# The causal convolution of a hybrid decoder layer, with tokens on the partitions

## Chip, cores and metric

One core of a Trainium2 chip runs the whole program. The metric is the device time of one execution in microseconds (us), lower is better; the kernel before takes 1735.56 us (median of 3 runs, 1734.17 to 1737.68). The engines are PE (TensorE, matmuls and transposes), DVE (VectorE), ACT (ScalarE), POOL (GpSimd) and SP (SyncE, which here only issues transfers). Sixteen DMA engines move data. SBUF is the on-chip memory with 128 partitions, PSUM the one that PE writes.

## What is computed

Two layers on x of 256 tokens by 2048 features. What the change touches is the convolution group.

```python
h = _rmsnorm(x, norm_pre) * (1.0 + scale[:, None, :]) + shift[:, None, :]
z = h @ w_in                                  # 2048 x 14336
gb, gcin, u, g_c, q, k, v, g_r = jnp.split(z, offs, axis=-1)

y_conv = gb * _causal_short_conv(gcin * u, conv_w)   # sum of w[k] * up[:, k:k + s], 3 taps over tokens
y_conv = y_conv * jax.nn.silu(g_c)
...                                           # rope, retention with 8 heads, GroupNorm, silu(g_r): y_ret
o = jnp.concatenate([y_conv, y_ret], axis=-1) @ w_out
return x + gate[:, None, :] * _rmsnorm(o, norm_post)
```

All data are float32. The scale, shift and gate come from silu(c) @ w_ada, also with 2048 x 6144 weights a layer.

## The kernel before

**Weights.** The work is a list of chunks `CH`. A chunk is 512 weight rows by 512 columns (1 MB; the 35 chunks at the front are of other sizes). SP loads it into one of 4 slots of `stage` (L528 to L545), in an order fixed by `load_table`; a slot is loaded again once what was in it is used. ACT casts each half chunk to float32r, `w_hi` (`cast`, L569), DVE subtracts to get the rest, `w_lo` (`low`, L744), and PE forms three products for each pair of tiles (`products`, L1162 to L1164): activations and weights are both split in a high and a low part. `w_hi` and `w_lo` are rings of 4 half chunks, so a cast waits for PE's products of two chunks before. Slots of `stage` also take parts of `w_ada`, 1 MB each, that DVE multiplies and adds itself (`ada_chunk`, L763 and L765): in turns 1, 2 and 3 for layer 1, and in the output projections.

**Turns.** The columns of `w_in` are worked through in 4 turns a layer, 8 in all (t = 0 to 7), each with 512 columns of each of 7 blocks (q and k, v, g_r, g_c in, u, g, gb), 28 chunks a turn, 4 to a block. Layer 0's turn 0 is spread over the front. Beside the products of a chunk each engine runs one small piece of the turn, chosen by a hand-written timetable: `Steps_at` holds for each piece at which chunk, counted from the turn's first, it stands in each engine's program. `USUAL` is for turns 1 to 7, `FIRST` for turn 0. A step above 27 lies in the chunks of the next turn (or of the output projection). All engines run their programs in order, and at every chunk an engine does first the cast, `low` or products of that chunk, then a `w_ada` part where there is one, and then the pieces of that step. In turn 0 the steps count from chunk 28, so steps 7 and on lie beside turn 1's first chunks.

**The convolution.** `z` has tokens on the partitions (tile i has tokens 128 i to 128 i + 127), in PSUM, or in `part` for turn 0. In order:
- `cu` (DVE, step 21; 8 in turn 0): u times g_c in, into `R2` (or `part`), still by tokens.
- `trc` (PE, 21; 9): eight 128x128 transposes into PSUM bank B (A in turn 0), so that features are on partitions and tokens along the row.
- `y0` (ACT, 23; 11): last tap into `R4`, four activations with a scale for each partition (L721). In turn 0 it waits for `s_in`, the products of the retention (PE's `inner`, step 9), as in the others.
- `conv` (DVE, 24; 12): the taps one and two tokens back, eight multiply-adds on shifted rows (L1038).
- `sg` (ACT, 25; 9) silu(g) and `gate` (DVE, 29; 10) gb times it, by tokens, in `R2`; `trg` (PE, 29; 21): eight transposes of that.
- `ymul` (DVE, 31; 23): gate times convolution, in `R4`; `yhi` (ACT, 32; 24) and `ylo` (DVE, 33; 25) split it into `YC` for the output projection.

The steps of the retention lie between: `rope` 5, `p` 9, `inner` 9, `stats` 11, `yn` 13 and so on. `R4` also takes the retention's scores `p` from turn 2 on.

Of the kernel before, what the change touches and what calls it, by code (L numbers as in the profile page):

```python
# [10 lines left out]
F32 = mybir.dt.float32  # L11
# [53 lines left out]
def chunk_table():  # L65
# [7 lines left out]
    for l in range(LAYERS):  # L73
# [5 lines left out]
        for nb in range(NB):  # L79
            for w in range(OUT_CH):  # L80
# [39 lines left out]
                for kc in range(tiles)]  # L120
# [15 lines left out]
                      " gcopy cu trc y0 conv sg gate trg ymul yhi ylo")  # L136
# [83 lines left out]
def build(nc, x, c, positions, norm_pre, norm_post, w_ada, b_ada, w_in, conv_w, gn_gain, w_out,  # L220
          consts, decay, out):
    ctx = ExitStack()
    with ctx:
# [62 lines left out]
        front_stage, _ = place("front_stage", [P, SLOTS, CK, BLK], F32, at_yr)  # L286
        c_cols, _ = place("c_cols", [P, KT, COL], F32, at_r4)
# [69 lines left out]
        s_trc = sem("cu_transposed")  # L357
        s_y0 = sem("conv_last_tap")
# [100 lines left out]
        def cu_bank(t):  # L459
            return four(A if t == 0 else B)  # L460
# [100 lines left out]
        def _(act):  # L561
# [77 lines left out]
            for n, ch in enumerate(CH):  # L639
# [35 lines left out]
                for t in turn_of(n):  # L675
# [8 lines left out]
                    if s == at.v and t > 0:  # L684
                        act.wait_ge(s_pe, z_done(t, VV))
                        act.wait_ge(s_in, t)
                        N.copy(v_sb[:, :, :], z_of(t, VV)).then_inc(taken(t, VV)[0], 1)
# [7 lines left out]
                    if s == at.yn:  # L695
                        act.wait_ge(s_rs, t + 1)
                        act.wait_ge(s_trq, t + 1)
                        for q in range(4):
                            h, i = divmod(q, 2)
                            ins = N.activation(yn_buf(t)[:, i, h * DV:(h + 1) * DV], B[:, h, i * DV:(i + 1) * DV],  # L700
                                               ACT.Identity, bias=nb4[:, q:q + 1], scale=rs4[:, q:q + 1])
                        ins.then_inc(s_yn, 1)
                    if s == at.yrhi:
# [10 lines left out]
                    if s == at.y0:  # L714
                        act.wait_ge(s_trc, t + 1)
                        act.wait_ge(s_in, t + 1)
                        if t:
                            act.wait_ge(s_ylo, t)
                        for e in range(TILES):
                            w = PRM_CW + 48 * (t // TURNS) + KT * (CONV_K - 1) + 4 * (t % TURNS) + e  # L720
                            ins = N.activation(R4[:, e, :], cu_bank(t)[:, e, :], ACT.Copy, scale=prm[:, w:w + 1])  # L721
                        ins.then_inc(s_y0, 1)
# [14 lines left out]
        def _(dve):  # L737
# [108 lines left out]
            def x_end(i):  # L846

                dve.wait_ge(s_xsq, 2 + 2 * i + 2)
                variance(xsq[:, i, :], NT + i)

# [54 lines left out]
            for n, ch in enumerate(CH):  # L905
# [68 lines left out]
                for t in turn_of(n):  # L974
# [58 lines left out]
                    if s == at.conv:  # L1033
                        dve.wait_ge(s_y0, t + 1)
                        for back in (1, 2):
                            for e in range(TILES):
                                w = PRM_CW + 48 * (t // TURNS) + KT * (CONV_K - 1 - back) + 4 * (t % TURNS) + e
                                ins = V.scalar_tensor_tensor(R4[:, e, back:S], cu_bank(t)[:, e, 0:S - back],  # L1038
                                                             prm[:, w:w + 1], R4[:, e, back:S], ALU.mult, ALU.add)
                                if back == 1:  # L1040
                                    me.then(ins)
                            if back == 1:
                                me.wait()
                        ins.then_inc(s_cv, 1)
                    if s == at.gate:
                        if t == 0:
                            dve.wait_ge(s_fin, fin(GB))
                        else:
                            dve.wait_ge(s_pe, z_done(t, GB))
                            dve.wait_ge(s_trc, t + 1)  # L1050
                        dve.wait_ge(*taken(t, GG))
                        V.tensor_tensor(gate_buf(t), z_of(t, GB), sg_buf(t), ALU.mult).then_inc(taken(t, GB)[0], 1)
                    if s == at.ymul:
                        dve.wait_ge(s_trg, t + 1)
                        dve.wait_ge(s_cv, t + 1)
                        V.tensor_tensor(R4[:, :, :], gate_bank(t), R4[:, :, :], ALU.mult).then_inc(s_ym, 1)
                    if s == at.ylo:
                        dve.wait_ge(s_yhi, t + 1)
                        k = slice(4 * (t % TURNS), 4 * (t % TURNS) + 4)
                        V.tensor_tensor(YC[:, k, S:2 * S], R4[:, :, :], YC[:, k, 0:S].bitcast(F32), ALU.subtract)\  # L1060
                            .then_inc(s_ylo, 1)
# [7 lines left out]
        def _(pool):  # L1069
# [42 lines left out]

            for t in range(ALL_TURNS):
                pool.wait_ge(s_mv, t + 1)
                if t:
                    pool.wait_ge(s_yn, t)
# [15 lines left out]
        def _(pe):  # L1132
# [111 lines left out]
            for n, ch in enumerate(CH):  # L1244
# [32 lines left out]
                for m, at_n in enumerate(ADA_SUM):  # L1277
                    if n == at_n:
# [3 lines left out]
                        if s < USUAL.scores:  # L1282
                            pe.wait_ge(s_ym, t)
# [12 lines left out]
                for t in turn_of(n):  # L1296
                    at, s = steps(t), n - base(t)
                    if s == at.trq:
                        pe.wait_ge(s_rope, t + 1)
                        if t == 0:  # L1300
                            pe.wait_ge(s_tmp, group_units(0, GROUPS - 1))
                        else:
                            pe.wait_ge(s_cv, t)
                            pe.wait_ge(s_yn, t)
                        if t == TURNS:
                            pe.wait_ge(s_tmp, group_units(1, GROUPS - 1))
                        turned(four(B), tok(R1)).then_inc(s_trq, 1)
# [30 lines left out]
                    if s == at.trc:  # L1338
                        pe.wait_ge(*taken(t, UU))
                        if t:  # L1340
                            pe.wait_ge(s_yn, t + 1)
                        else:
                            pe.wait_ge(s_p, 1)
                        if t == 1:
                            pe.wait_ge(s_ym, 1)
# [42 lines left out]
```

## Time and profile before

| | |
|---|---|
| median of 3 runs | 1735.56 us (1734.17 to 1737.68) |
| the profiled execution's own time | 1735.0 us |
| its span, first to last instruction | 1733.1 us |
| TensorE's granted clock, mean | 0.995 of full |
| PE, DVE, ACT busy | 1696.5, 1130.0, 720.9 us |
| moved by DMA | 414.61 MB, 239 GB/s over the span |

The profile is of one execution. Busy times count instructions in execution; PE's matmuls are pipelined, so an instruction's time (0.39 us) is longer than the distance to the next (0.23 us). A row of a timeline gives start, duration, engine, line, operation, output and inputs and, in brackets, how long the engine was idle before and what released it. A row with "x4" is four instructions merged. Times from issue to landing are those of transfers.

### The profile page before, as it was taken

How to read it: one execution, taken by the hardware profiler on the slowest of the kernel's cores; microseconds unless marked ns; L12 is line 12 of the kernel's file. 1: busy time of each engine (PE TensorE's matmuls, PEld its weight loads, DVE VectorE, ACT ScalarE, POOL GpSimd, SP SyncE). 2: the span in 40 equal slices, each digit the busy share in tenths (PEclk: the TensorE clock that was granted, in tenths of full speed). 3: DMA queues.
4: the chain of work that ended last, by engine and by line, in shares of the span. 5: the costliest groups of instructions: out<-in, count | busy, mean ns of one | idle time of the engine just before them, and what ended most of it. 6: DMA issues, size and time to landing. Idle time of an engine off the chain costs nothing. (4 is left out here: it accounts for less than half of the span.)

```text
span 1733.1 us, 19029 instructions
## 1 busy us (share of the span) xinstructions
PE 1696.5 (98%) x7795; PEld 1385.5 (80%) x7795; DVE 1130.0 (65%) x1305; ACT 720.9 (42%) x814; POOL 40.9 (2%) x78
## 2 busy tenths in 40 slices
PE   5999999999999999999989999999999999999998
PEld 3667888888888888888868888888888888888886
DVE  2598766878787775677775545555554555467776
ACT  2333444443444444344354443444444444444332
POOL 4000000000000000000000000000000000000000
PEclk9999999999999999999999999999999999999999
DMA  9998545787878866777765555555555555568774
GB/s 341 383 379 307 190 165 195 250 290 269 296 269 290 291 235 233 267 281 282 279 226 170 177 194 188 176 180 191 194 176 194 185 184 173 188 234 298 285 281 186
DMA packets 227398, 414.61 MB, mean 239 GB/s; under 512 B 7520, under 2 KB 48880, under 8 KB 226544
## 3 DMA queue, kind: packets, MB, share of 16 engines
q1 hardware_dynamic: 225888, 408.97, 68.2%
q10 hardware_dynamic: 1424, 4.43, 0.6%
q8 instruction: 61, 1.00, 0.2%
q14 instruction: 25, 0.20, 0.0%
HBM read 411.28 MB, written 2.10 MB: 239 GB/s over the span
## 5 line engine op out<-in xcount | busy, mean ns | idle before, releaser
L744 DVE TENSOR_TENSOR w_lo<-stage,w_hi 128x1024 fp32r<-128x1024 f32 x574 | 692.7, 1222 | 519.7 <-ACT w_hi L569 517.9
L569 ACT CAST w_hi<-stage 128x1024 fp32r<-128x1024 f32 x574 | 596.4, 1051 | 947.0 <-PE Z L1164 605.5
L1162 PE MATMUL Z<-w_hi,H 128*128 128x512 f32 x1784 | 704.7, 395 | 8.5 <-DVE w_lo L744 5.8
L1164 PE MATMUL Z<-w_hi,H 128*128 128x512 f32 x1784 | 696.8, 391 | 0.0
L1163 PE MATMUL Z<-w_lo,H 128*128 128x512 f32 x1784 | 696.0, 390 | 0.0
L1162 PEld LDWEIGHTS Z<-w_hi,H 128*128 128x128 f32 x1784 | 336.1, 188 | 85.2 <-issue 11.8
L1164 PEld LDWEIGHTS Z<-w_hi,H 128*128 128x128 f32 x1784 | 335.7, 188 | 71.1
L1163 PEld LDWEIGHTS Z<-w_lo,H 128*128 128x128 f32 x1784 | 336.2, 188 | 67.8
L765 DVE SCALAR_TENSOR_TENSOR acc<-stage,c_silu,acc 128x512 f32<-128x512 f32 x240 | 180.1, 751 | 6.8
L1162 PE MATMUL Z<-w_hi,YC 128*128 128x512 f32 x256 | 102.3, 400 | 0.0
L1162 PE MATMUL Z<-w_hi,YR 128*128 128x512 f32 x256 | 100.8, 394 | 0.0
L1164 PE MATMUL Z<-w_hi,YC 128*128 128x512 f32 x256 | 99.8, 390 | 0.0
L1163 PE MATMUL Z<-w_lo,YC 128*128 128x512 f32 x256 | 99.8, 390 | 0.0
L1163 PE MATMUL Z<-w_lo,YR 128*128 128x512 f32 x256 | 99.7, 390 | 0.0
L1164 PE MATMUL Z<-w_hi,YR 128*128 128x512 f32 x256 | 99.7, 389 | 0.0
L1162 PEld LDWEIGHTS Z<-w_hi,YR 128*128 128x128 f32 x256 | 48.1, 188 | 11.3 <-issue 0.9
L1163 PEld LDWEIGHTS Z<-w_lo,YC 128*128 128x128 f32 x256 | 48.1, 188 | 11.3 <-issue 1.4
L1162 PEld LDWEIGHTS Z<-w_hi,YC 128*128 128x128 f32 x256 | 48.1, 188 | 11.2 <-issue 1.4
L1163 PEld LDWEIGHTS Z<-w_lo,YR 128*128 128x128 f32 x256 | 48.1, 188 | 10.3 <-issue 0.5
L1164 PEld LDWEIGHTS Z<-w_hi,YR 128*128 128x128 f32 x256 | 48.1, 188 | 10.1
L1164 PEld LDWEIGHTS Z<-w_hi,YC 128*128 128x128 f32 x256 | 48.1, 188 | 10.1
L918 DVE TENSOR_TENSOR part<-Z,part 128x1024 f32<-128x1024 f32 x27 | 32.9, 1220 | 3.8 <-PE Z L1164 3.8
(141 smaller groups left out, 684.8 us busy)
## 6 DMA issues: line engine op xcount, KB each, us to landing
stage<-in_w_in SPq DMA_DIRECT2D x186, 1024.0 KB, 5.2
stage<-in_w_ada SPq DMA_DIRECT2D x64, 1024.0 KB, 7.5
stage<-in_w_out SPq DMA_DIRECT2D x64, 1024.0 KB, 7.4
stage<-in_w_in SPq DMA_DIRECT2D x74, 512.0 KB, 5.5
front_stage<-in_w_ada SPq DMA_DIRECT2D x32, 1024.0 KB, 11.5
xt<-in_x SPq DMA_DIRECT2D x2, 1024.0 KB, 6.6
dec<-decay SPq DMA_DIRECT2D x8, 256.0 KB, 5.5
rows<-in_b_ada ACTq DMA_DIRECT2D x2, 1024.0 KB, 7.7
```

The costliest lines, as they stand in the source:

```text
L569: N.copy(w_bufs(n, h)[0], stage[:, slot_of(n), 2 * h:2 * h + 2, :]).then_inc(s_hi, 1)
L744: V.tensor_tensor(lo, stage[:, slot_of(n), 2 * h:2 * h + 2, :], hi.bitcast(F32), ALU.subtract)\
L765: ins = V.scalar_tensor_tensor(acc[:, :], w, c_silu[:, k:k + 1], acc[:, :], ALU.mult, ALU.add)
L918: V.tensor_tensor(dst, Z[m % 2][:, :, :], part[:, was.b, :, :], ALU.add).then_inc(s_fin, 1)
L1162: T.matmul(z[:, i, :], hh, wh, start=ch.first and a == 0, stop=False)
L1163: T.matmul(z[:, i, :], hh, wl, start=False, stop=False)
L1164: ins = T.matmul(z[:, i, :], hl, wh, start=False, stop=stop)
```

## The change

The convolution stays with tokens on partitions. A shift by one or two tokens is then a shift by partitions; it is done by transfers within SBUF, issued by ACT at step `back`. There are two for each shift: one for rows within the two token tiles (127 or 126 partitions of 4 KB), and one for the one or two rows that cross from tile 0 to tile 1. The first rows of tile 0 are zeroed by GpSimd. The three taps of the turn's 512 channels are loaded to all 128 partitions (ACT, step 13, or 2 in turn 0: three transfers of 256 KB written) and DVE multiplies and adds them at three steps `tap`. `gate` and `ymul` then work by tokens, and only their result is transposed (`trg`), then split as before. `trc` and `y0` are gone. The moved copies lie in `YC` (turn 0: in `YR`), the taps in `YR`, `v_sb` and `acc2`.

```diff
-                 tr=14, yrhi=16, yrlo=17, gcopy=17, cu=21, trc=21, y0=23, conv=24, sg=25, gate=29, trg=29,
-                 ymul=31, yhi=32, ylo=33)
+                 tr=14, yrhi=16, yrlo=17, gcopy=17, cu=21, back=22, tap=(22, 24, 25), sg=25, gate=29,
+                 ymul=30, trg=30, yhi=32, ylo=33)
 FIRST = Steps_at(rope=2, radd=3, trq=4, qkt=6, v=3, scores=6, p=8, inner=9, stats=11, sgr=7, yn=13, mult=13,
-                 tr=17, yrhi=19, yrlo=20, gcopy=99, cu=8, trc=9, y0=11, conv=12, sg=9, gate=10, trg=21,
-                 ymul=23, yhi=24, ylo=25)
+                 tr=17, yrhi=19, yrlo=20, gcopy=99, cu=8, back=9, tap=(9, 11, 12), sg=9, gate=10,
+                 ymul=15, trg=21, yhi=23, ylo=24)
...
+                    if s == (at.yn if t else 2):
...
+                        for k in range(CONV_K):
+                            row = conv_w[t // TURNS, k, j * BLK:(j + 1) * BLK]
+                            dst = taps[j][:, k, :] if j < TURNS - 1 else v_sb[:, k, :] if k < 2 else acc2[:, :]
+                            act.dma_start(dst, row.partition_broadcast(P)).then_inc(s_taps, 16)
...
-                    if s == at.y0:
-                        act.wait_ge(s_trc, t + 1)
...
+                    if s == at.back:
+                        act.wait_ge(*taken(t, UU))
+                        act.wait_ge(s_zero, t + 1)
+                        cu, b = cu_buf(t), behind_buf(t)
+                        for n_back in (1, 2):
+                            to = b[:, n_back - 1, :, :]
+                            act.dma_start(to[n_back:P, :, :], cu[0:P - n_back, :, :]).then_inc(s_back[n_back - 1], 16)
+                            act.dma_start(to[0:n_back, 1, :], cu[P - n_back:P, 0, :]).then_inc(s_back[n_back - 1], 16)
...
                     if s == at.yhi:
-                        act.wait_ge(s_ym, t + 1)
-                        N.copy(YC[:, 4 * (t % TURNS):4 * (t % TURNS) + 4, 0:S], R4[:, :, :]).then_inc(s_yhi, 1)
+                        act.wait_ge(s_trg, t + 1)
+                        N.copy(YC[:, 4 * (t % TURNS):4 * (t % TURNS) + 4, 0:S], gate_bank(t)).then_inc(s_yhi, 1)
...
+            def conv_tap(t, n_back):
+
+                row, b = tap_row(t, CONV_K - 1 - n_back), behind_buf(t)
+                if n_back == 0:
+                    dve.wait_ge(s_taps, 16 * CONV_K * (t + 1))
+                    dve.wait_ge(s_in, t + 1)
+                    if t:
+                        dve.wait_ge(s_trg, t)
+                    dve.wait_ge(*taken(t, UU))
+                    me.then(V.tensor_tensor(tok(R4), cu_buf(t), row, ALU.mult))
+                    return
+                at_ = b[:, n_back - 1, :, :]
+                dve.wait_ge(s_back[n_back - 1], 32 * (t + 1))
+                me.then(V.tensor_tensor(at_, at_, row, ALU.mult))
+                me.wait()
+                ins = V.tensor_tensor(tok(R4), tok(R4), at_, ALU.add)
...
-                        dve.wait_ge(s_trg, t + 1)
+                        dve.wait_ge(*taken(t, GB))
                         dve.wait_ge(s_cv, t + 1)
-                        V.tensor_tensor(R4[:, :, :], gate_bank(t), R4[:, :, :], ALU.mult).then_inc(s_ym, 1)
+                        V.tensor_tensor(tok(R4), gate_buf(t), tok(R4), ALU.mult).then_inc(s_ym, 1)
...
             for t in range(ALL_TURNS):
                 pool.wait_ge(s_mv, t + 1)
+                if t:
+                    zeros(t)
...
-                            pe.wait_ge(s_cv, t)
                             pe.wait_ge(s_yn, t)
+                        if t > 1:
+                            pe.wait_ge(s_ylo, t - 1)
...
-                            pe.wait_ge(s_ym if t > 1 else s_cv, t)
+                            pe.wait_ge(s_ylo if t > 1 else s_p, t)
...
-                    if s == at.trc:
...
-                        turned(cu_bank(t), cu_buf(t)).then_inc(s_trc, 1)
                     if s == at.trg:
-                        pe.wait_ge(*taken(t, GB))
+                        pe.wait_ge(s_ym, t + 1)
...
-                        turned(gate_bank(t), gate_buf(t)).then_inc(s_trg, 1)
+                        turned(gate_bank(t), tok(R4)).then_inc(s_trg, 1)
```

## Rows read from the trace of the kernel before

**Rows 1.** The page's busy times: us, share of the span, instructions.
```profile
PE 1696.5 (98%) x7795; PEld 1385.5 (80%) x7795; DVE 1130.0 (65%) x1305; ACT 720.9 (42%) x814; POOL 40.9 (2%) x78
```

**Rows 2.** The page's chain that ended last, shares of the span by engine.
```profile
PE 47%; issue 1%; DVE 0%; POOL 0%; DVEq 0%; ACT 0%; POOLq 0%
```

**Rows 3.** Waits of PE for w_lo: us in total, times, longest.
```profile
PE Z L1162 <- DVE w_lo L744: 5.8, 2, 4.6
```

**Rows 4.** Timeline of PE, cu transposes of turn 4: start us, us.
```profile
1032.59 1.03 PE L1228 MATMUL B<-ident,R 128*128 128x128 f32 x8
1033.38 0.48 PE L1162 MATMUL Z<-w_hi,H 128*128 128x512 f32 x1
1033.70 0.40 PE L1163 MATMUL Z<-w_lo,H 128*128 128x512 f32 x1
```

**Rows 5.** Instructions by line and form: busy us, mean ns, idle before.
```profile
L1038 DVE SCALAR_TENSOR_TENSOR R<-B,prm,R 128x254 f32<-128x254 f32 x28 | 11.6, 475 | 0.2
L721 ACT ACTIVATE R<-B,prm 128x256 f32<-128x256 f32 x28 | 10.9, 474 | 0.0
L1017 DVE TENSOR_TENSOR R<-R,R 128x1024 f32<-128x1024 f32 x7 | 8.5, 1218 | 0.0
```

**Rows 6.** Timeline of DVE in turn 0, steps 9 to 11.
```profile
231.22 1.23 DVE L744 TENSOR_TENSOR w_lo<-stage,w_hi 128x1024 fp32r<-128x1024 f32 x1 [1.44 <-ACT w_hi L569]
233.99 1.22 DVE L744 TENSOR_TENSOR w_lo<-stage,w_hi 128x1024 fp32r<-128x1024 f32 x1 [1.54 <-ACT w_hi L569]
...
243.60 1.43 DVE L1007 BATCH_NORM_STATS2 stats<-B 128x6 f32<-128x256 f32 x4 [0.29 <-PE B L1329]
```

**Rows 7.** Timeline of PE behind step 9 of turn 0.
```profile
243.40 1.04 PE L1228 MATMUL A<-ident,part 128*128 128x128 f32 x8
```

**Rows 8.** ACT, second cast of step 9 of turn 0.
```profile
230.13 1.05 ACT L569 CAST w_hi<-stage 128x1024 fp32r<-128x1024 f32 x1 [1.61 <-PE Z L1164]
```

**Rows 9.** Turn 4: ACT's second cast of step 22, w_lo of 25.
```profile
1027.35 1.05 ACT L569 CAST w_hi<-stage 128x1024 fp32r<-128x1024 f32 x1 [1.61 <-PE Z L1164]
...
1044.60 2.35 DVE L744 TENSOR_TENSOR w_lo<-stage,w_hi 128x1024 fp32r<-128x1024 f32 x2
```

**Rows 10.** Timeline of PE in turn 4: step 25 begins at 1049.80.
```profile
1049.12 0.39 PE L1162 MATMUL Z<-w_hi,H 128*128 128x512 f32 x1
...
1049.80 0.39 PE L1162 MATMUL Z<-w_hi,H 128*128 128x512 f32 x1
```

**Rows 11.** DMA issues: KB, median us to landing; one on ACT's queue.
```profile
stage<-in_w_in SPq DMA_DIRECT2D x186, 1024.0 KB, 5.2
...
718.92 0.45 ACTq L660 DMA_DIRECT2D rows<-in_norm_post  x1
```

**Rows 12.** A stretch (DMA share, GB/s last); the loads' queue.
```profile
360.00:370.00 10.00, 10.00 (x46) 8.29 (x45) 9.03 (x15) 4.70 (x5) 0.00 (x0) 1.00 1.05 391
...
q1 hardware_dynamic: 225888, 408.97, 68.2%
```

**Rows 13.** Casts, w_lo of step 22, PE at 25, turns 1 and 2.
```profile
350.29 2.00 ACT L569 CAST w_hi<-stage 128x1024 fp32r<-128x1024 f32 x2 [4.12 <-DMA stage<-in_w_in]
...
373.03 0.39 PE L1162 MATMUL Z<-w_hi,H 128*128 128x512 f32 x1
...
513.33 1.23 DVE L744 TENSOR_TENSOR w_lo<-stage,w_hi 128x1024 fp32r<-128x1024 f32 x1 [0.70 <-ACT w_hi L569]
...
535.21 0.39 PE L1162 MATMUL Z<-w_hi,H 128*128 128x512 f32 x1
```

**Rows 14.** SP's issues in turn 1, steps 22 to 24.
```profile
357.19 0.51 SPq L525 DMA_DIRECT2D stage<-in_w_ada  x1
362.13 0.92 SPq L545 DMA_DIRECT2D stage<-in_w_in  x2
```

**Rows 15.** DVE's w_lo and PE's start at step 4 of turn 2.
```profile
411.26 2.36 DVE L744 TENSOR_TENSOR w_lo<-stage,w_hi 128x1024 fp32r<-128x1024 f32 x2 [2.81 <-ACT w_hi L569]
...
412.63 0.47 PE L1162 MATMUL Z<-w_hi,H 128*128 128x512 f32 x1
```

More of the change, by code:

```diff
@@ L135 @@
 Steps_at = namedtuple("Steps_at", "rope radd trq qkt v scores p inner stats sgr yn mult tr yrhi yrlo"
-                      " gcopy cu trc y0 conv sg gate trg ymul yhi ylo")
+                      " gcopy cu back tap sg gate ymul trg yhi ylo")
 USUAL = Steps_at(rope=5, radd=6, trq=6, qkt=8, v=9, scores=7, p=9, inner=9, stats=11, sgr=13, yn=13, mult=14,
-                 tr=14, yrhi=16, yrlo=17, gcopy=17, cu=21, trc=21, y0=23, conv=24, sg=25, gate=29, trg=29,
-                 ymul=31, yhi=32, ylo=33)
+                 tr=14, yrhi=16, yrlo=17, gcopy=17, cu=21, back=22, tap=(22, 24, 25), sg=25, gate=29,
+                 ymul=30, trg=30, yhi=32, ylo=33)
 FIRST = Steps_at(rope=2, radd=3, trq=4, qkt=6, v=3, scores=6, p=8, inner=9, stats=11, sgr=7, yn=13, mult=13,
-                 tr=17, yrhi=19, yrlo=20, gcopy=99, cu=8, trc=9, y0=11, conv=12, sg=9, gate=10, trg=21,
-                 ymul=23, yhi=24, ylo=25)
+                 tr=17, yrhi=19, yrlo=20, gcopy=99, cu=8, back=9, tap=(9, 11, 12), sg=9, gate=10,
+                 ymul=15, trg=21, yhi=23, ylo=24)
 ALL_TURNS = LAYERS * TURNS
@@ L286, in build @@
         front_stage, _ = place("front_stage", [P, SLOTS, CK, BLK], F32, at_yr)
+        taps = [place(f"taps{j}", [P, CONV_K, BLK], F32, at_yr + 4 * 2 * S * 4 * (j + 1) + (0 if j else 4 * 2 * S * 4))[0]
+                for j in range(TURNS - 1)]
+        behind = [place(f"behind{j}", [P, 2, NT, BLK], F32, at_yc + 4 * 2 * S * 4 * j)[0] for j in range(TURNS)]
+        behind_0, _ = place("behind_0", [P, 2, NT, BLK], F32, at_yr + 4 * 2 * S * 4)
         c_cols, _ = place("c_cols", [P, KT, COL], F32, at_r4)
@@ L356, in build @@
         s_cu = sem("cu_done")
-        s_trc = sem("cu_transposed")
-        s_y0 = sem("conv_last_tap")
+        s_taps = sem("conv_taps_loaded")
+        s_zero = sem("first_tokens_zeroed")
+        s_back = [sem(f"cu_moved_back{n}") for n in (1, 2)]
         s_cv = sem("conv_done")
@@ L457, in p_buf, with behind_buf, tap_row @@
             return at[:, 0:2 * 3 * P].rearrange("p (h s) -> p h s", h=2)
-        def cu_bank(t):
-            return four(A if t == 0 else B)
+        def behind_buf(t):
+            return behind[t % TURNS] if t else behind_0
+        def tap_row(t, k):
+            row = taps[t % TURNS][:, k, :] if t % TURNS < TURNS - 1 else v_sb[:, k, :] if k < 2 else acc2[:, :]
+            return row.rearrange("p (o f) -> p o f", o=1).broadcast_to([P, NT, BLK])
         def gate_bank(t):
@@ L686, in _ @@
                         act.wait_ge(s_in, t)
+                        if t == TURNS:
+                            act.wait_ge(s_cv, t)
                         N.copy(v_sb[:, :, :], z_of(t, VV)).then_inc(taken(t, VV)[0], 1)
@@ L713, in _ @@
                         N.copy(gc_buf(t), z_of(t, GC)).then_inc(taken(t, GC)[0], 1)
-                    if s == at.y0:
-                        act.wait_ge(s_trc, t + 1)
[L716 to L722, printed above, removed]
+                    if s == at.back:
[6 more added lines that the diff above has]
+                            act.dma_start(to[0:n_back, 1, :], cu[P - n_back:P, 0, :]).then_inc(s_back[n_back - 1], 16)
                     if s == at.sg:
@@ L849, in x_end @@
                 variance(xsq[:, i, :], NT + i)
+            def conv_tap(t, n_back):
[13 more added lines that the diff above has]
+                ins = V.tensor_tensor(tok(R4), tok(R4), at_, ALU.add)
+                if n_back == CONV_K - 1:
+                    ins.then_inc(s_cv, 1)
+                else:
+                    me.then(ins)
             def front_rows(k, kc):
@@ L1032, in _ @@
                         V.tensor_tensor(cu_buf(t), z_of(t, UU), gc_buf(t), ALU.mult).then_inc(taken(t, UU)[0], 1)
[L1033 to L1044, printed above, removed]
+                    for n_back in range(CONV_K):
+                        if s == at.tap[n_back]:
+                            conv_tap(t, n_back)
                     if s == at.gate:
@@ L1049, in _ @@
                             dve.wait_ge(s_pe, z_done(t, GB))
-                            dve.wait_ge(s_trc, t + 1)
+                            dve.wait_ge(s_cv, t + 1)
                         dve.wait_ge(*taken(t, GG))
@@ L1111, in _, with zeros @@
             pool.sem_inc(s_tab, 1)
+            def zeros(t):
+                for n_back in (1, 2):
+                    ins = G.memset(behind_buf(t)[0:n_back, n_back - 1, 0, :], 0.0)
+                    if n_back == 1:
+                        me.then(ins)
+                me.wait()
+                ins.then_inc(s_zero, 1)
+            pool.wait_ge(s_ga, len(FRONT_GROUPS))
+            zeros(0)
             for t in range(ALL_TURNS):
                 pool.wait_ge(s_mv, t + 1)
+                if t:
+                    zeros(t)
                 if t:
@@ L1282, in _ @@
                         if s < USUAL.scores:
-                            pe.wait_ge(s_ym, t)
+                            pe.wait_ge(s_ylo, t)
                         elif s < USUAL.tr:
```

14 lines of the change are left out of this document (6 added, 8 removed).

## The prediction

> **What bounds the kernel now.** I read the busy times first [rows 1]: the tensor engine (PE) works 1696.5 of 1733.1 us, VectorE (DVE) 1130.0, ScalarE (ACT) 720.9. The chain that ended last agrees [rows 2]: of the 48% of the span that it puts down to anything, 47 are PE's, so time goes away only where PE does less, and comes only where PE is made to wait. The list of waits shows how well PE is fed [rows 3]: its longest entry is 5.8 us on w_lo in the whole run. What the reader is to take along is the feeding line: SP loads a chunk of weights into one of 4 stage slots, ACT casts it to w_hi, DVE subtracts to w_lo, PE multiplies. Three products take 0.68 us [rows 10], so a chunk of 24 takes 5.44 us, and the ring of 4 half chunks lets DVE be one to two chunks ahead. DVE runs its program in order; whatever blocks it for longer than its lead stops PE. So I compared, chunk by chunk, when w_lo was ready and when PE began.
>
> **Removed from PE.** The eight transposes of cu, once in each of 8 turns. Between the last product before them and the normal rhythm behind them lie 1032.59 to 1033.38, and the first product behind is 0.08 us slow [rows 4]: 0.87 us, nothing beside it. 8 x 0.87 = 7.0 us. The other transposes stay; they read R4 in place of gate_buf. All of the 7.0 is on PE's path, since PE is the bound in all eight places.
>
> **Changed on DVE and ACT.** DVE drops 8 multiply-adds a turn (8 x 0.41 of pitch, 3.3 us) and gets three multiplies and two adds of 128x1024. An operation of that shape from SBUF is 1.22 us by itself and 1.14 behind another [rows 5]; with two waits on its own result 1.14 + 2.4 + 2.4 = 5.9 us, so 2.6 us more a turn, spread over steps 22, 24 and 25. ACT drops four ACTIVATEs (1.6 us) and issues seven transfers at up to 0.45 us each, 3.2 us [rows 11]. In an undisturbed turn both hide: in turn 4 DVE has finished the weights of step 25 4 us before PE wants them (1045.8 against 1049.80) [rows 9, 10]. The tap loads (768 KB a turn) are issued 9 steps ahead. GpSimd's two memsets stand before the head statistics, which ACT wants some 8 us after they are ready. Waiting for s_ylo in place of s_ym or s_cv, and the product (ymul) ahead of the transposes instead of behind, changes order inside two or three steps of 5.4 us where DVE is ahead. I cost these at nothing; if the cover is gone the price is what DVE has more, up to 2.6 us a turn.
>
> **Turn 0: a wait that is new.** tap 0 stands at step 9 and waits for s_in, which PE gives only behind the products of that very step. Before, the first reader of s_in stood at step 11. DVE finishes the weights of step 9 at 232.4, and its first reader of s_in starts at 243.6 only [rows 6]. Behind the waiting instruction is the w_lo of the next chunk, made at 235.2 before [rows 6]. Now: 243.60 + 1.14 (tap 0) + 1.22 and 0.1 until PE starts are 246.1, while PE is free at 243.40 [rows 7]: 2.7 us lost. Two steps on, the three taps, head statistics and rope pile up (from 244.7 two w_lo, the gate product, two w_lo and 1.8 us of statistics make 252.3; tap 1 of 2.4, two w_lo, tap 2 of 2.4, rope of 2.3 and a w_lo reach 262.9, against 262.6 of PE): with 0.1 to start again 0.5 us more.
>
> **The moves, the disputed cost.** Each turn ACT issues, behind the casts of step 22 (step 9 in turn 0), a move of 127 partitions x 4 KB and one of 126. DVE wants the first at step 24 (11 in turn 0). The trace has no transfer within SBUF and none with such a partition count: its transfers have 128, 48 or 16 partitions, all divisible by 16. So I bound it. Lower end: spread evenly like the loads. A 1024 KB load lands in 5.2 us [rows 11], at 391 GB/s its bytes are 2.7 us [rows 12], so 2.5 us is fixed; the moves would land in some 5 to 8 us and DVE, which comes two steps (11 us) later, never waits. Upper end: 127 is prime, so the only way to cut it in equal runs of partitions is one run, on one of the sixteen engines: 520,192 bytes at 391/16 = 24.4 GB/s are 21.3 us, 16 times its even share. I take the upper end, because every transfer seen is one that cuts into 16 equal parts and with all sixteen at work (share 1.05), and for 127 the equal cut is one.
>
> A page of the Trainium skill bears on this and speaks against the change: "DMA: Bandwidth & Descriptors", section "Why a DMA increments its semaphore by 16 and not by 1", has an HWDGE transfer run on the largest number of engines up to 16 that divides its slowest dimension, and names 127 partitions as a case of one engine. By that rule the time is the 1862 below, without it 1734. No row of the trace can show it; that its 128-partition loads fill all sixteen engines agrees. The section "Queues, rings and completion order" has each engine alternate between queues packet by packet, which would make the move, the larger, land after the weights that share its engine, as I count next.
>
> On that one engine also lies a sixteenth of every weight load, 64 KB or 2.7 us. In which order it serves them the trace doesn't show; I count in full the loads issued until DVE stops, since each is an eighth of the move and any even turn-taking finishes it first, and bound this below. **Turn 4**, standing for 3 to 7: the second cast of step 22 ends at 1028.4, the issue at 1028.9; fixed 2.5, own bytes 21.3, three loads (released by w_lo of steps 22, 23, 24) 8.1: landed 1060.8. Then tap 1, 2.4, and one w_lo, 1.2: 1064.4. PE wants it at 1049.80 - 0.87 = 1048.9 [rows 9, 10]. Lost 15.4 us, five times 77.0. Behind the waiting tap lie DVE's w_lo, behind them PE, and SP, whose slots are then full, so that the line recovers within the turn; I add no later stall. **Turn 1**: five loads are under way, one of them for w_ada [rows 13, 14]. 352.3 + 0.45 + 2.5 + 21.3 + 13.5 + 3.6 = 393.7 against 373.03 - 0.87 = 372.2: 21.5 us. **Turn 2** the same way from 513.3, also five loads, two for w_ada: 554.7 against 534.3: 20.3 us [rows 13]. **Turn 0** [rows 8]: 231.2 + 0.45 + 2.5 + 21.3 + three loads and the decay tile 8.8 = 264.2; + 3.6 = 267.8, where PE, after the 2.7 us, wants it at 257.1: 10.7, and the pile behind grows to 1.4. With the 2.7, 14.8 us. Sum: 77.0 + 21.5 + 20.3 + 14.8 = 133.6. With the 7.0 saved: +126.6 on the profiled execution's own 1735.0, which is 0.6 below the median: **1862 us** (1861.6).
>
> **Bounds of that.** If the loads don't hold up the move (no 8.1, 13.5, 8.8), the losses are 7.3 x 5, 8.0, 6.8 and 6.0 = 57.3: 1785 us. A rate 10% lower (the whole run's mean for a busy engine: 408.97 MB over 68.2% of 16 x 1733 us, 21.6 GB/s [rows 12]) adds 2.8 x 8 = 22; one more load each adds another 22: 1906. Below 1785 I allow three microseconds less each, if an engine alone is faster than one of sixteen at work: 1760.
>
> **Rivals.**
> 1. Even spread, no change. The moves land in time. -7.0, +3.2 in turn 0, and the stretch of turns 1 and 2 that is fed from the w_ada loads: there the w_lo that starts at 411.26 is ready at 412.48, and PE, free at 412.5, begins with it [rows 15]. The 1.1 us of tap 0 and 1 MB of moves beside the loads of steps 22 to 25 delay the slot of each next load by up to 4, tap 2 adds 2.4 at step 25: some 2.2 us there and 0.4 in turn 2. Sum -1.2: 1734. For it: 68% DMA share leaves room. Against: 127.
> 2. Even spread, faster, the other side. The same, but the lead of 3 to 4 us in turns 1 and 2 covers DVE's 2.6 us. Only turn 0's 3.2 us stay: -3.8, 1731 us. It decides if the moves land within the two steps and don't push the loads of steps 22 to 25 back by over 1 us.
> 3. Even spread, but transfers within SBUF at half the pace: 5.4 us of all engines more in the three turns with w_ada and gate loads, in stretches at share 1.0: three times 2 to 3 us, +6: 1741, slower.
> 4. The change doesn't do what it says: the transposes left aren't fewer. The diff takes the whole group out, so I give this nothing.
>
> **How the numbers follow.** One engine 0.82 (all slower, with or without the loads' share), rival 1 0.09, rival 2 0.05, rival 3 0.04. Faster by over 0.2% (3.5 us, about what a measurement of this kernel tells from no change) 0.05, within 0.2% 0.09, slower 0.86. The range is that of the likeliest case, 1760 to 1900, and leaves out the even cases (0.18) and a few hundredths of its tail.
>
> **What would show it.** Right: in each turn DVE idles before the first add or multiply with the tap one token back, released by a transfer on ACT's queue, for 12 to 25 us; that transfer lands 25 to 40 us after its issue, the 126-partition one shortly behind; PE waits for w_lo behind it, at eight places 150 us apart; 64 fewer transposes; in turn 0 DVE idles to 243.6 before tap 0. DMA share falls to near a sixteenth in the stalls. Wrong: moves that land in under 10 us (the placing failed, 1731 to 1741), or landings near 24 us, which would show that weight loads don't hold the move up (1785). If PE then waits at steps 2 to 6 of turn 2, rival 1's tight stretch is the cause.

## The result and the profile after

The changed kernel takes 1855.1 us (median; 1853.4 to 1859.1) where the kernel before took 1736.6 beside it: ratio 1.069, 95% interval 1.068 to 1.071, 118.5 us slower. 1862 was forecast. The profiled execution, the slowest of the four, has a span of 1857.3 us, against 1733.1 before.

The page of the changed kernel: busy times (answers to [rows 1]), PE's granted clock in tenths over 40 slices, and the chain that ended last (answers to [rows 2]).

```profile
PE 1732.6 (93%) x7731; PEld 1406.7 (76%) x7731; DVE 1147.9 (62%) x1281; ACT 705.5 (38%) x782; POOL 51.5 (3%) x94
...
PEclk9999989989998999999989998999999899989999
...
PE 40%; DMA 6%; DVE 1%; issue 0%; ACTq 0%; DVEq 0%; POOL 0%; POOLq 0%; ACT 0%
```

PE does 64 instructions fewer and yet is busy 36 us longer; a transfer now has 6% of the chain, 7 slices fall below 9 in the clock, and PE works 93% of the span instead of 98. The list of waits (us in total, times, longest) names who waits:

```profile
ACT w_hi L580 <- issue: 97.0, 7, 14.8
...
PE Z L1210 <- DVE w_lo L767: 93.5, 19, 8.1
...
DVE behind L887 <- DMA behind<-R: 73.4, 7, 11.3
...
DVE behind L887 <- DMA behind<-part: 6.2, 1, 6.2
```

The second line answers to [rows 3]: 5.8 us in two places have become 93.5 in 19. The third and fourth were forecast: DVE waits for the move, eight times. The first was not: ACT stands still for 97 us over seven turns (and for 13.4 us in turn 0), and its releaser is "issue", which here are DMA issues of its own. Turn 4 shows what that is. ACT's timeline (L744 issues the large transfer, L745 the small one):

```profile
1093.85 0.65 ACTq L744 DMA_DIRECT2D behind<-R  x1
1094.53 11.55 ACTq L745 DMA_DIRECT2D behind<-R  x1
1106.11 0.92 ACTq L744 DMA_DIRECT2D behind<-R  x1
1107.06 1.63 ACTq L745 DMA_DIRECT2D behind<-R  x1
1108.79 3.88 ACT L580 CAST w_hi<-stage 128x1024 fp32r<-128x1024 f32 x4 [13.95 <-issue]
```

The transfer of 127 rows is issued in 0.65 us, but the small one behind it takes 11.55 us to issue, and all of ACT's casts stand behind that. DVE in the same turn:

```profile
1109.87 4.63 DVE L767 TENSOR_TENSOR w_lo<-stage,w_hi 128x1024 fp32r<-128x1024 f32 x4 [12.63 <-ACT w_hi L580]
1124.76 1.23 DVE L887 TENSOR_TENSOR behind<-behind,taps 128x1024 f32<-128x1024 f32 x1 [10.27 <-DMA behind<-R]
1126.02 1.23 DVE L889 TENSOR_TENSOR R<-R,behind 128x1024 f32<-128x1024 f32 x1
1127.17 2.35 DVE L767 TENSOR_TENSOR w_lo<-stage,w_hi 128x1024 fp32r<-128x1024 f32 x2
```

DVE is starved twice: 12.63 us by ACT, and 10.27 us by the move, which lands 1124.76 - 1093.85 = 30.9 us after its issue. PE stops twice as well, at the first products of step 23 and of step 25, which start at

```profile
1111.15 0.80 PE L1210 MATMUL Z<-w_hi,H 128*128 128x512 f32 x1 [6.52 <-DVE w_lo L767]
...
1128.44 0.79 PE L1210 MATMUL Z<-w_hi,H 128*128 128x512 f32 x1 [3.21 <-DVE w_lo L767]
```

Stretches of the same place (from:to, length, busy time and instructions of PE, PEld, DVE, ACT and POOL, granted clock of PE, DMA share, GB/s):

```profile
1111.00:1117.00 6.00, 5.85 (x14) 4.60 (x15) 3.50 (x4) 1.95 (x3) 0.00 (x0) 0.50 0.64 209
1117.00:1125.00 8.00, 8.00 (x36) 6.42 (x34) 0.24 (x1) 3.79 (x4) 0.00 (x0) 0.98 0.40 129
1125.00:1129.00 4.00, 0.79 (x2) 0.50 (x2) 3.96 (x4) 1.04 (x1) 0.00 (x0) 0.82 0.06 22
1129.00:1134.00 5.00, 5.00 (x13) 3.90 (x12) 4.97 (x5) 0.00 (x0) 0.00 (x0) 0.50 0.66 210
```

In the third row one engine of sixteen is at work (a share of 0.06, 22 GB/s). From 1124.3 to 1126.2 it moves 9 of the 126 rows, a fourteenth of them, and then its share of a load of weights. Behind each stop PE, having stood idle, is granted 0.50 (1.2 GHz, the lower level) for the first 6 us of its work. A product then comes every 0.43 us instead of 0.23; the first twelve of step 23 take 2.6 us longer than at full clock.

What a turn loses I measure as the distance from PE's first w_hi product of turn 4's step 10 to that of turn 5. After:

```profile
1032.58 0.58 PE L1210 MATMUL Z<-w_hi,H 128*128 128x512 f32 x1
...
1207.64 0.58 PE L1210 MATMUL Z<-w_hi,H 128*128 128x512 f32 x1
```

That is 175.06 us. Before, the same two stand at 966.14 and 1126.10, 159.96 apart. With the 0.9 us that the transposes gave back (below), the moves cost 16.0 us in this turn: 6.7 and 3.4 of standing still (against the usual distance of products), and 3.0 and 2.9 in the two half chunks behind each stop, nearly all of it at half clock.

### The profile page after: what moved, and what is told of

The parts are those of the page before. It is cut to its first block and busy times, and to the rows that moved or that the text cites. A ratio compares the mean times of both kernels' runs of the same rounds, so it can differ in the third digit from the quotient of the medians.

```text
span 1857.3 us, 18925 instructions
## 1 busy us (share of the span) xinstructions
PE 1732.6 (93%) x7731; PEld 1406.7 (76%) x7731; DVE 1147.9 (62%) x1281; ACT 705.5 (38%) x782; POOL 51.5 (3%) x94
## 5 line engine op out<-in xcount | busy, mean ns | idle before, releaser
L1210 PE MATMUL Z<-w_hi,H 128*128 128x512 f32 x1784 | 722.4, 405 | 96.3 <-DVE w_lo L767 93.5
L1211 PE MATMUL Z<-w_lo,H 128*128 128x512 f32 x1784 | 710.1, 398 | 0.0
L1212 PE MATMUL Z<-w_hi,H 128*128 128x512 f32 x1784 | 709.0, 397 | 0.0
L1210 PEld LDWEIGHTS Z<-w_hi,H 128*128 128x128 f32 x1784 | 345.1, 193 | 184.1 <-DVE w_lo L767 94.3
L1212 PEld LDWEIGHTS Z<-w_hi,H 128*128 128x128 f32 x1784 | 344.5, 193 | 75.0
L1211 PEld LDWEIGHTS Z<-w_lo,H 128*128 128x128 f32 x1784 | 345.7, 194 | 70.3
L1211 PEld LDWEIGHTS Z<-w_lo,YC 128*128 128x128 f32 x256 | 48.1, 188 | 11.3 <-issue 1.4
L1210 PEld LDWEIGHTS Z<-w_hi,YC 128*128 128x128 f32 x256 | 48.1, 188 | 11.3 <-issue 1.4
L887 DVE TENSOR_TENSOR behind<-behind,taps 128x1024 f32<-128x1024 f32 x12 | 14.7, 1222 | 57.8 <-DMA behind<-R 51.6
```

The lines of the kernel that those rows point to most:

```text
L887: me.then(V.tensor_tensor(at_, at_, row, ALU.mult))
L1210: T.matmul(z[:, i, :], hh, wh, start=ch.first and a == 0, stop=False)
L1211: T.matmul(z[:, i, :], hh, wl, start=False, stop=False)
L1212: ins = T.matmul(z[:, i, :], hl, wh, start=False, stop=stop)
```

## The experiments

All edits are against the changed kernel unless said otherwise; all change when something happens and not what is computed. The theory: the 127 rows can't be cut in equal runs of partitions, so they go through one DMA engine, and everything lost follows from that. The rivals: transfers within SBUF are slow as such; a large transfer is slow whatever its row count; the issue that blocks ACT is the cause, rather than the landing; the loads of weights are what really comes late.

**1. Both moves cut into 112 rows and the rest.**

```
-    act.dma_start(to[n_back:P, :, :], cu[0:P - n_back, :, :])...
+    act.dma_start(to[n_back:n_back + 112, :, :], cu[0:112, :, :])...
+    act.dma_start(to[n_back + 112:P, :, :], cu[112:P - n_back, :, :])...
...
-    dve.wait_ge(s_back[n_back - 1], 32 * (t + 1))
+    dve.wait_ge(s_back[n_back - 1], 48 * (t + 1))
```

> Each move is cut in two pieces that divide evenly: 112 partitions and the 15 or 14 left; everything else is as in the changed kernel. Theory A (the 127-partition move runs on one of the sixteen engines, and both the block of ACT's queue and DVE's wait come from that): no issue on ACT's queue over 2 us, DVE doesn't idle before its tap one token back, and the time is the sum without the moves, 1735.0 - 7.0 + 3.2 (wait for s_in in turn 0) + 2.6 (turns 1 and 2) = 1734, between 1730 and 1740. Theory B (transfers within SBUF, or several in a row on ACT's queue, are slow whatever their shape): the stalls stay and the time is above 1800, since two more transfers a turn are issued.

Measured: 1736.6 us, ratio to the kernel before 1.0009 (1.0000 to 1.0018). One more issue for each move and the same bytes take away the whole loss. The page's transfers (KB each, median us to landing):

```profile
behind<-R ACTq DMA_DIRECT2D x14, 448.0 KB, 3.6
```

448 KB within SBUF land in 3.6 us in the median, less than the 5.2 of a load of 1024 KB, so transfers within SBUF aren't slow. No issue on ACT's queue is over 1.4 us: the block goes with the one engine. PE's waits for w_lo are

```profile
PE Z L1211 <- DVE w_lo L768: 12.0, 7, 4.9
```

The longest stands at the front, as before. Turn 0 has a new one of 2.5 us behind the wait for s_in. Of the rest three count: PE loses 1.05 us at step 26 of turn 1 and 0.58 and 2.09 at steps 25 and 26 of turn 2. At steps 2 to 6 of turn 2, the stretch that rival 1 named, it doesn't stop: the 0.85 us more at step 3 are the eight transposes of the gated result, which the change has put there.

**2. Only the 127 rows cut** (112 and 15; the two-token move stays whole with 126 rows).

> The changed kernel with the one-token move alone cut, into 112 and 15 rows; the two-token move stays whole, 126 rows. If only the 127 rows are at fault, this is the kernel with even moves: 1734 to 1740 us, the 126 rows landing within 4 to 8 us. If a transfer of all rows in one piece is slow whatever their number, the two-token move still lands some 20 us or more after its issue, and a stall stays ahead of its tap: 1770 us or more.

Measured: 1736.5 us, ratio 1.0009 (0.9999 to 1.0018), the same as with both cut. So the row count is at fault and not the size, and only that of one transfer. DVE waits for the 126 rows in no turn. In turn 4 its second tap (1053.17) stands 16.1 us behind their issue at 1037.07, and the last packet of ACT's queue starts before 1046.6: up to 9.5 us, a little over the 4 to 8 expected.

**3. The 127 rows cut into 122 and 5.** 122 is 2 x 61, so by the theory two engines carry 61 rows each.

```
-    act.dma_start(to[n_back:P, :, :], cu[0:P - n_back, :, :])...
+    if n_back == 1:
+        act.dma_start(to[1:123, :, :], cu[0:122, :, :])...
+        act.dma_start(to[123:P, :, :], cu[122:P - 1, :, :])...
+    else: (as before)
```

> Only the move by one token is recut, in 122 partitions (a number whose largest divisor up to 16 is 2) and 5. Theory A in its general form (the number of engines is the largest divisor up to 16): 61 rows of 4 KB on each of two engines are 10.2 us at 24.4 GB/s, landed 16 to 20 us after the issue with the loads between. The block of ACT's queue falls from 11.6 us to about half, DVE waits 0 to 4 us, and the time is 1740 to 1775. If instead any count that isn't a multiple of 16 goes to one engine, it stays at 1850; if only a prime does, it is near e1_even's.

Measured: 1768.7 us, ratio 1.019 (1.017 to 1.021), inside the range. ACT's queue:

```profile
1050.68 0.64 ACTq L745 DMA_DIRECT2D behind<-R  x1
1051.36 0.76 ACTq L746 DMA_DIRECT2D behind<-R  x1
1052.15 0.96 ACTq L749 DMA_DIRECT2D behind<-R  x1
```

and DVE's first use of the moved rows:

```profile
1070.71 1.23 DVE L891 TENSOR_TENSOR behind<-behind,taps 128x1024 f32<-128x1024 f32 x1 [6.91 <-DMA behind<-R]
```

Landing 20.0 us after the issue, at the edge of what was expected; the wait of 6.91 us is longer than the 0 to 4. That the queue would be blocked for half as long was wrong: it isn't blocked at all. The block therefore isn't in proportion to the rows.

**4. The 127 rows cut into 97 and 30.** 97 is prime.

> The changed kernel with the one-token move cut into 97 rows (a prime number, so by the reading so far all on one engine) and 30 rows (divisible by 15), all else left alone. The 97 rows are 97/127 of the bytes on the one engine: 16.3 us instead of 21.3 of its own bytes, and by the ratio of the measured 31 us a landing 23.7 us after the issue. The stall ahead of step 25 by the move alone is then 10.05 - 7.2 = some 3 to 4 us a turn where ScalarE's queue isn't blocked, with half clock behind it 5 to 6 us, so 1765 to 1790 us. If ScalarE's queue is blocked by rows that stand on one engine above some number between 61 and 97, an issue behind it is long (11.6 us less the 7 us by which the move is shorter: 4 to 5 us); if it is blocked only above 97, all issues are below 1.4 us.

Measured: 1825.8 us, ratio 1.052 (1.050 to 1.054), 36 us above the range. Queue and landing in turn 4:

```profile
1078.20 0.66 ACTq L745 DMA_DIRECT2D behind<-R  x1
1078.89 4.29 ACTq L746 DMA_DIRECT2D behind<-R  x1
...
1104.89 1.23 DVE L891 TENSOR_TENSOR behind<-behind,taps 128x1024 f32<-128x1024 f32 x1 [11.44 <-DMA behind<-R]
```

The block of 4.29 us is the 4 to 5 expected for a limit between 61 and 97 rows. The traces show that limit more closely. From the start of the large issue to the end of the blocked one ACT's queue moved (packets, MB, share), for 127 rows in the changed kernel and for 97 here,

```profile
q10 hardware_dynamic: 46, 0.19, 4.9%
...
q10 hardware_dynamic: 16, 0.07, 4.6%
```

A packet here is one row of 4 KB. The blocked issue ends when 46 of 127 or 16 of 97 rows have gone, with 81 left each time (in the other turns 76 to 86, where it can be counted); 61 rows on an engine are below that from the start. The landing is 26.7 us and not 23.7: scaling the whole 31 us by 97/127 was wrong, since only the move's own bytes scale. The prediction's own sum has it: 2.5 + 21.3 x 97/127 + 8.1 = 26.9. And I had taken 7.2 us off the two stops, leaving out the half clock behind them.

**5. The same four transfers, the 127 rows issued last.**

```
-    for n_back in (1, 2):
+    for n_back in (2, 1):
         to = b[:, n_back - 1, :, :]
-        act.dma_start(to[n_back:P, :, :], cu[0:P - n_back, :, :])...
         act.dma_start(to[0:n_back, 1, :], cu[P - n_back:P, 0, :])...
+        act.dma_start(to[n_back:P, :, :], cu[0:P - n_back, :, :])...
```

> The four transfers of a turn are issued in the other order: the small ones and the 126-partition move first, the 127-partition move last. Nothing is issued behind it, so ACT goes on to its casts. It tells what the blocked queue costs beside the late landing. Theory A1 (the landing sets the end; the block only brings part of the loss forward): the stall at step 23 goes, the one at step 25 grows from 3.4 us to 12 to 16 in turn 4, and the time is 1830 to 1860. Theory C (the blocked queue is the larger cost): the stalls at step 23 (46 us and some 17 us at half clock behind them) go and those at step 25 stay: 1780 to 1800.

Measured: 1889.8 us, ratio 1.089 (1.087 to 1.091): above both theories' ranges, and slower than the changed kernel. The order of issue is now small, 126 rows (L745), small, 127 rows (L745). ACT's queue and DVE's tap in turn 4:

```profile
1107.99 0.82 ACTq L745 DMA_DIRECT2D behind<-R  x1
1108.84 0.57 ACTq L744 DMA_DIRECT2D behind<-R  x1
1109.44 1.08 ACTq L745 DMA_DIRECT2D behind<-R  x1
...
1142.92 1.23 DVE L887 TENSOR_TENSOR behind<-behind,taps 128x1024 f32<-128x1024 f32 x1 [22.50 <-DMA behind<-R]
```

Nothing is issued behind the 127 rows, no issue is long, and the stop at step 23 is gone. The stop at step 25 has taken its place and grown to 17.8 us: the landing, 33.5 us after the issue, ends it in any case. So the block was no cost of its own; it brought forward a part of a loss that the landing sets. The rest is the order. The 127 rows are issued 2.2 us later than they were (1109.44 - 1107.28, the turn's first issue) and stand behind 126 rows, of which this engine gets a fourteenth (seen above): 36 KB, 1.5 us at 24.4 GB/s, an estimate.

**6. The changed kernel, its moves issued by GpSimd.**

```
     act: (the four dma_start of a turn and their two waits, taken out)
+    pool: (the same, behind the turn's memsets and head statistics; in turn 0 behind the memsets)
```

> The changed kernel with nothing altered but the queue: the four moves of a turn are issued by GpSimd, which has no other work at that time, instead of by ScalarE. Theory A, the transfer of 127 rows is placed on one DMA engine whatever queue issues it: the landing stays near 31 to 34 us after the issue. ScalarE's own casts are then not held up, so the stall ahead of step 23 goes, but the loads go on beside the move, as where the 127 rows were issued last, and the one stall ahead of step 25 grows to 15 to 18 us: 1850 to 1890 us. Theory B, the placing belongs to ScalarE's queue: landings of 4 to 8 us, no stall, 1734 to 1745 us.

Measured: 1745.0 us, ratio 1.005 (1.003 to 1.007): theory B, at its upper end. The page's transfers, and the queue's kind, packets, MB and share:

```profile
q0 software_dynamic: 2816, 8.34, 1.9%
...
behind<-R POOLq DMA_DIRECT2D x7, 508.0 KB, 6.0
behind<-R POOLq DMA_DIRECT2D x7, 504.0 KB, 6.9
```

The same 127 rows, uncut, land in 6.0 us, where 31 are needed through ACT's queue. From turn 4 on a turn takes 159.07 us as with even moves. What keeps this version 8 us above experiment 1 lies in turns 1 and 2 (168.0 and 166.9 us from step 10 to step 10, against 164.0 and 163.6), where ACT waits 8.98 us for a load at step 23 of turn 1; why the load is later there was not tried.

**7. Nothing faster, the users later.** The kernel of experiment 5 with

```
-    ... tap=(22, 24, 25), sg=25, gate=29,
-    ymul=30, trg=30, yhi=32, ylo=33)
+    ... tap=(22, 29, 30), sg=25, gate=30,
+    ymul=31, trg=31, yhi=32, ylo=33)
```

> The kernel in which the 127 rows are issued last (1889.8 us, landing 34 us after its issue, ScalarE's queue not held), with nothing made faster but the users of the move put later: the one-token and two-token taps at steps 29 and 30 instead of 24 and 25 in turns 1 to 7, the gate at step 30 instead of 29, the product and the transposes of the gated result at step 31 instead of 30. Theory A, the move costs time only because its taps stand in VectorE's queue ahead of the splits of weights: the landing (34 us is 6.3 steps of 5.44 us) is then over at step 28.3, the stalls of 17 to 18 us ahead of step 25 go, and what is left is turn 0 (12 to 15 us, not altered) and the late loads of turns 1 and 2 (7 us each with half clock behind): 1745 to 1775 us. Theory B, the move also holds up the loads of weights, so that the stall stays or moves elsewhere: 1830 us or more.

Measured: 1806.0 us, ratio 1.041 (1.039 to 1.043), between the theories and in neither range. Both hold, each in its stretch. Of the 72 us more than in experiment 1, 12.9 lie ahead of step 10 of turn 1, 22.8 in turn 1, 15.6 in turn 2, 12.4 in turn 3 with the output stage behind it and 8.2 in the last stretch; none in turns 4 to 6. PE's first products of step 10 of turns 5 and 6:

```profile
1193.32 0.58 PE L1210 MATMUL Z<-w_hi,H 128*128 128x512 f32 x1
...
1352.35 0.58 PE L1210 MATMUL Z<-w_hi,H 128*128 128x512 f32 x1
```

159.03 us: there a transfer of over 30 us costs nothing at all. In turn 1, where w_ada's loads come on top, ACT shows the other half:

```profile
386.06 1.99 ACT L580 CAST w_hi<-stage 128x1024 fp32r<-128x1024 f32 x2 [12.80 <-DMA stage<-in_w_in]
402.19 1.99 ACT L580 CAST w_hi<-stage 128x1024 fp32r<-128x1024 f32 x2 [14.14 <-DMA stage<-in_w_in]
```

Here it isn't a tap that DVE waits for: the loads themselves come late. Those issued from 360 to 405 us land in

```profile
stage<-in_w_in SPq DMA_DIRECT2D x6, 1024.0 KB, 16.2
```

where 5.2 is the median before. A sixteenth of each passes the engine that carries the move. In turn 5 the same lateness is 6.24 us at one cast, and the ring covers it. So the move has two prices: the tap that waits for it, and the loads that share its engine. The second is hidden where the loads have slack.

**8. Even moves, tap 0 of turn 0 free of s_in.** Experiment 1 with the wait for s_in (tap 0 writes into R4, which is the retention's operand from turn 2 on) taken out of turn 0:

```
-    dve.wait_ge(s_in, t + 1)
     if t:
+        dve.wait_ge(s_in, t + 1)
         dve.wait_ge(s_trg, t)
```

> As e1_even, and tap 0 of turn 0 no longer waits for s_in (there R4 isn't the retention's operand). By the working of the prediction this wait costs 2.7 us and 0.5 behind it: 3.2 us less than e1_even, near 1731, and DVE's idle time to 243.6 us is gone. If the moves or the taps' loads fill that place with another wait, it is the same as e1_even.

Measured: 1734.1 us, ratio 0.9991 (0.9982 to 1.0000); 2.5 us less than experiment 1 by the medians of 11 runs each (3.2 by the means, give or take 1.8). DVE's idle time to 243.6 is gone.

**9. The taps apart as well** (experiment 8 with tap=(21, 24, 27)).

> The kernel with even moves and tap 0 free, with tap 0 put at step 21 and the one-token and two-token taps at steps 24 and 27 instead of 22, 24 and 25, so that no two taps stand close together on VectorE. With the taps close, four small stalls were left (0.96, 0.81 and 2.07 us at half chunks 61, 66 and 89), each with some products at half clock behind it. If these come from taps that stand too close, they go, and the time is 1729 to 1731 us, 0.3% below the kernel before. If they come from weights that land late, they stay, and the time is 1733 to 1735 us.

Measured: 1730.6 us, ratio 0.9967 (0.9955 to 0.9979): the stops at step 26 of turns 1 and 2 are gone, and the change is now worth having, by 0.33%. Two short stops are left in turn 2, 0.66 us at step 2, in the stretch that rival 1 named, and 0.58 at step 27. PE's waits for w_lo are 1 us below experiment 8's 9.0, against 5.8 in [rows 3]:

```profile
PE Z L1211 <- DVE w_lo L768: 8.0, 5, 4.7
```

**Turn 4 across the runs.** Landing: from the start of the transfer's issue to DVE's tap. Sum: the prediction's 2.5 + 21.3 x rows/127 + 8.1, and 1.5 more in the last line. Turn: between PE's first products of step 10, as above. Loss: the turn less 159.06.

| largest part on one engine | issue blocked, us | landing, us | sum, us | turn, us | loss, us |
|---|---|---|---|---|---|
| 61 rows (exp. 3) | none | 20.0 | 20.8 | 163.06 | 4.0 |
| 97 rows (exp. 4) | 4.3 | 26.7 | 26.9 | 169.58 | 10.5 |
| 127 rows (the change) | 11.6 | 30.9 | 31.9 | 175.06 | 16.0 |
| 127 rows, last (exp. 5) | none | 33.5 | 33.4 | 179.17 | 20.1 |

Landing less loss is 16.0, 16.2 and 14.9 us, and 15.5 in the last line if counted from the turn's first issue (35.6): nearly one number, with a block or without. The landing sets the loss, and the distance to the tap is the slack that it uses up first.

## Why the prediction came out as it did

**The placing: right.** The disputed cost was taken from its upper end, one engine. Experiments 1 to 4 settle it by row counts: 127 and 97 rows behave as one engine, 122 as two, 126 and 112 as many; the DMA share of 0.06 shows the one engine at work. The rule of the Trainium skill that was weighed there ("DMA: Bandwidth & Descriptors", section "Why a DMA increments its semaphore by 16 and not by 1") gives 1, 1, 2, 14 and 16 engines for these, and the traces agree: landings of 30.9, 26.7, 20.0 and, for 112, 3.6 us, and 9 of the 126 rows on one engine. The same section has an exception that I had not weighed: a transfer issued by GpSimd may be spread over sixteen engines whatever its count. Experiment 6 agrees, with 6.0 us for 127 rows.

**The landing: right in size and in its terms.** From the start of the issue the sum 0.45 + 2.5 + 21.3 + 8.1 = 32.4 met 30.9 in turn 4; in turns 0, 1 and 2 it was 33.0, 37.8 and 37.8 and met 30.1, 35.0 and 34.4. The table shows what the sum is made of: beyond 2.5 and the move's own bytes there are 7.3, 7.9 and 7.1 us for 61, 97 and 127 rows, an amount that doesn't grow with the rows, as it should be if it is other work on the engine. The bound of 1785 (loads that don't hold up the move, 24 us) is out. The loads issued between the move and its landing in turn 4 are (KB each, median us to landing)

```profile
stage<-in_w_in SPq DMA_DIRECT2D x2, 1024.0 KB, 13.3
stage<-in_w_in SPq DMA_DIRECT2D x2, 512.0 KB, 9.7
```

3 MB, the three loads of the prediction; it is the same in experiments 3, 4 and 5. What is left over of the sum is mostly the rate. Where the engine works for the move alone, stretch and queue read

```profile
1110.00:1113.00 3.00, 1.85 (x4) 1.49 (x5) 3.00 (x3) 2.67 (x3) 0.00 (x0) 0.50 0.06 26
q10 hardware_dynamic: 19, 0.08, 6.3%
```

26 GB/s, and not a sixteenth of 391, so that 127 rows are 20.0 us and 30.9 - 2.5 - 20.0 = 8.4 are left for the loads, against 8.1. The even turn-taking that the prediction assumed shows too: from 1102 to 1106 that engine takes 17 packets of the move and 17 of a load.

**The single stall at step 25: wrong in form.** The prediction costed ACT's issues at up to 0.45 us each, from [rows 11], and saw one stop a turn. The issue behind the 127 rows took 11.55 us, so that ACT, and not the move, stopped the line first, at step 23. It was still right in size, since the block replaces a part of the later stop (experiment 5). For the same reason DVE's idle time before the tap was not the 12 to 25 us named as a sign of being right, but 6.2 to 11.3. Had I worked out the block as one more cost, I would have been some 7 us a turn too high.

**Half clock: left out.** The sum counted standing still only: 15.4 us by the start of step 25 in turn 4. By then 13.1 were lost (6.7 + 3.0 + 3.4), and 2.9 more came behind it, since PE runs at 0.50 after each stop. 16.0 against 15.4: two errors of 2 to 3 us that nearly cancel. So close a match was luck.

**Turns 0 to 2: over-counted.** Predicted 14.8, 21.5 and 20.3. Compared with the kernels with even moves, turn 1 is 182.16 - 163.99 = 18.2 us longer and turn 2 179.42 - 163.64 = 15.8; for turn 0 there are 2.5 ahead of step 10 and 49.70 - 42.98 = 6.7 behind it, 9.2. The larger part of this is the landings, each put 2.8 to 3.4 us too late, 1.3 of it by the rate. Turn 0's tap by itself was right: DVE stands 11.21 us until 243.59, as forecast from [rows 6],

```profile
243.59 1.22 DVE L883 TENSOR_TENSOR R<-part,taps 128x1024 f32<-128x1024 f32 x1 [11.21 <-PE B L1378]
```

and experiment 8 puts its price at 2.5 us, where 2.7 and, with the pile behind it, 3.2 were forecast.

**The transposes: right.** 0.87 us a turn forecast from [rows 4]; 159.96 - 159.06 = 0.90 measured between the kernel before and experiment 1.

**Costed at nothing.** From turn 4 on, that holds: with even moves a turn has its 159.06 us, and DVE's extra 2.6 us hide. In turns 1 and 2 it doesn't quite: rival 1 gave 2.2 us for late loads and the pile of taps behind turn 1 and 0.4 in turn 2; with even moves PE lost 1.05 us at step 26 of turn 1, nothing at steps 2 to 6 of turn 2, and 2.7 at its steps 25 and 26 (0.58 and 2.09). Experiment 9 makes the two stops at step 26 go by moving the taps, so these were the taps' own pile. Rival 1's 1734 met 1736.6; rival 2's 1731 came out only with the taps apart and tap 0 freed, at 1730.6.

**The whole.** 133.6 of stalls less 7.0 were forecast, +126.6. The medians differ by 118.5, the spans of the two profiled executions by 124.2, from PE's step 10 to step 10 of the next turn as follows (forecast less the 0.87 of the transposes):

| stretch | forecast, us | measured, us |
|---|---|---|
| up to step 10 of turn 1 | 13.9 | 10.5 |
| turn 1 | 20.6 | 18.7 |
| turn 2 | 19.4 | 18.0 |
| turn 3 and the output stage | 14.5 | 19.3 |
| turns 4, 5 and 6 | 43.6 | 44.2 |
| the rest | 14.5 | 13.6 |

Turn 3 was priced as turn 4, but its two stops are 6.0 and 5.8 us where those of turn 4 are 6.7 and 3.4. Why wasn't tried, and the total owes some of its closeness to this: it makes up for most of what turns 0 to 2 were over-counted.

**A misread list.** The prediction calls 5.8 us on w_lo the longest entry of PE's waits. The list has a longer one, at the front:

```profile
PE Z L1234 <- DMA R<-in_conv_w: 11.1, 1, 11.1
```

The change leaves that alone (11.0 after), so nothing in the sum hangs on it.

## What to carry to other kernels

Before moving rows between partitions, look at the row count, not at the bytes: on ScalarE's queue 127 rows of 4 KB took 31 us, and cut into 112 and 15 the larger part took 3.6 in the median. An uneven shift should be cut into a part that divides by 16 and a rest, at the price of one issue of under 1.4 us. A transfer that is much longer than its neighbours is to be priced in three places: its user, the engine that issues what comes behind it, and the loads that share its DMA engine; if it can't be made short, put its users later, which hides it wherever the loads have slack. And where a stall is forecast for a tensor engine that was never idle, add the half clock behind it, here 2.9 us a stop.

## What the hardware showed that I had not expected

- Issuing on ScalarE's queue can itself block. Behind a transfer with 127 rows on one engine the next small one took 11.6 us to issue (13.9 in turn 1), behind 97 rows 4.3, behind 61 rows on each of two engines 0.8. In turns 0 and 6 the small one still got through and the 126 rows behind it were blocked (11.3 and 11.7 us). All of ScalarE's work waits behind it. Wherever it can be counted the block ended with 76 to 86 of the rows left; whether the limit counts rows or bytes was not tried.
- The same transfer is placed differently by the queue that issues it: 127 rows land in 31 us from ScalarE and in 6.0 us from GpSimd.
- Transfers within SBUF are quick when spread: 448 KB in 3.6 us, where a load of 1024 KB takes 5.2 [rows 11].
- Taking the block away by the order of issue made the kernel 34.7 us slower (1889.8 against 1855.1): what ScalarE gained at step 23 it had no use for, and the move it had to wait for anyway came later.
